# Second layer's gates and banded queries as two by two blocks with seven products

## What is computed

```python
def mixer_odd(h, hc, w_in, w_out, ml_gate_b, ml_norm_g, sw_sink, need_ctx):
    pl = split_cols(h @ w_in, ODD_SPLITS)
    pc = split_cols(hc @ w_in, ODD_SPLITS)
    ...
    oc_lat, oc_ctx = bidir_prefix(mlstm_scan, lat_f, ctx_f, lat_b, ctx_b, st0)
    yc = head_rmsnorm(oc_lat, ml_norm_g) * jax.nn.silu(pl[3])
    qd = axial_rope(heads(pl[5], SW_HEADS), rows, cols)
    kd = axial_rope(heads(pl[6], SW_KV_HEADS), rows, cols)
    ...
    od = swa_attn(qd, kd, vd, kdc, vdc, sw_sink)
    yd = merge(od) * jax.nn.silu(pl[8])
    y_lat = jnp.concatenate([yc, yd], axis=-1) @ w_out
```

## Time and profile before

| what | value |
|---|---|
| median of 3 runs | 1600.25 us (1599.61 to 1601.06) |
| profiled execution, span | 1600.2 us |
| PE busy | 1515.5 us (95%) |
| VectorE busy | 757.7 us (47%) |
| ScalarE busy | 570.1 us (36%) |
| GpSimd busy | 35.8 us (2%) |

### The profile page before, as it was taken

How to read it: one execution, slowest core, us unless ns; L and a number is a source line. 1 busy time by engine, 2 the same in 40 slices (tenths; PEclk the granted TensorE clock), 3 DMA queues, 4 the chain that set the end, 5 groups by cost and what they waited for, 6 DMA issues and landing times.

```text
span 1600.2 us, 25568 instructions
## 1 busy us (share of the span) xinstructions
PE 1515.5 (95%) x9656; PEld 1039.9 (65%) x9656; DVE 757.7 (47%) x1653; ACT 570.1 (36%) x1320; POOL 35.8 (2%) x108
## 2 busy tenths in 40 slices
PE   7999989999899899898999999999999999999996
PEld 4675876577467577564588866468574555556985
DVE  3144555423222322332577856245555655665776
ACT  0134355433332322443202342223334555554033
POOL 0000000000000000000000000000000010011000
PEclk9999999999999999999999999999999999999999
DMA  9200020240421412500334511222120200001443
GB/s 379 96 27 14 14 104 22 81 157 28 167 83 60 148 70 78 183 14 15 118 120 159 200 66 54 76 72 63 56 80 25 107 14 14 15 27 35 171 158 125
DMA packets 72037, 139.80 MB, mean 87 GB/s; under 512 B 6656, under 2 KB 44588, under 8 KB 70572
## 3 DMA queue, kind: packets, MB, share of 16 engines
q1 hardware_dynamic: 66604, 135.55, 24.0%
q10 hardware_dynamic: 5312, 2.62, 0.6%
HBM read 125.43 MB, written 12.71 MB: 86 GB/s over the span
## 4 chain that ended last, share of the span: by engine, by line
PE 76%; DVE 9%; issue 9%; ACT 4%; DMA 1%; SPq 0%; POOL 0%; DVEq 0%; ACTq 0%; POOLq 0%
PE proj L1250 16%; PE mixed L1250 14%; PE mixed L1234 4%; PE proj L1237 4%; PE turned L1358 4%; PE mixed L1200 4%; PE turned L1340 4%; PE proj L1234 3%; PE scores L1200 2%; ACT vstage L2095 2%; PE scores L1318 2%; PE mixed L1237 2%; PE scores L1321 2%; ACT work L2095 1%; PE scores L1250 1%
## 5 line engine op out<-in xcount | busy, mean ns | idle before, releaser
L1250 PE MATMUL proj<-hT,weights 128*128 128x512 f32 (+1 forms) x752 | 314.3, 564 | 3.0 <-ACT vstage L2095 2.1
L1250 PE MATMUL mixed<-hT,weights 128*128 128x512 f32 (+1 forms) x672 | 259.1, 534 | 1.5 <-DMA weights<-in_weights 0.9
L1250 PEld LDWEIGHTS proj<-hT,weights 128*128 128x128 f32 x752 | 138.3, 192 | 132.0 <-issue 128.2
L1250 PEld LDWEIGHTS mixed<-hT,weights 128*128 128x128 f32 x672 | 125.4, 194 | 100.6 <-issue 93.8
L2095 ACT ACTIVATE work<-turned 128x512 f32<-128x512 f32 (+2 forms) x136 | 72.7, 534 | 145.9 <-PE turned L1340 106.9
L1794 DVE TENSOR_TENSOR yT<-turned,work 128x128 f32<-128x128 f32 x72 | 21.0, 291 | 159.3 <-PE turned L1358 135.0
L2095 ACT ACTIVATE work<-work,stat 128x640 f32<-128x640 f32 (+8 forms) x98 | 74.0, 755 | 31.8 <-DVE stat L1765 29.8
L1340 PE MATMUL turned<-consts,work 128*128 128x128 f32 (+3 forms) x448 | 69.1, 282 | 10.9 <-DVE yT L1794 8.6
L1340 PEld LDWEIGHTS turned<-consts,work 128*128 128x128 f32 (+3 forms) x448 | 48.6, 139 | 42.9 <-issue 19.1
L1234 PE MATMUL mixed<-weights,hT 128*128 128x256 f32 x320 | 71.1, 379 | 0.0
L1234 PEld LDWEIGHTS mixed<-weights,hT 128*128 128x128 f32 x320 | 60.2, 190 | 9.0 <-issue 1.2
(11 more groups left out here) (343 smaller groups left out, 2590.1 us busy)
## 6 DMA issues: line engine op xcount, KB each, us to landing
weights<-in_weights SPq DMA_DIRECT2D x130, 512.0 KB, 3.9
tables<-in_bias SPq DMA_DIRECT2D x8, 1281.0 KB, 6.6
pair<-in_weights SPq DMA_DIRECT2D x20, 512.0 KB, 6.9
hT<-in_xT SPq DMA_DIRECT2D x8, 640.0 KB, 16.0
yT<-in_weights SPq DMA_DIRECT2D x8, 512.0 KB, 8.5
work<-in_xT SPq DMA_DIRECT2D x16, 256.0 KB, 2.8
x1T<-yT SPq DMA_DIRECT2D x8, 512.0 KB, 3.0
work<-rows SPq DMA_DIRECT2D x32, 128.0 KB, 3.4
```

What stands on the lines that cost most here:

```text
L1250: last = nc.tensor.matmul(PJ[BANK_OF[u]][:, 0:n], weights[:, w % WBUFS, k, :], src[:, k, t0:t0 + n], start=(k == 0), stop=(k == KT - 1))
```

## The change

The 12 tiles are taken in six pairs (`TILE_PAIRS`). For a pair, the weights A are two by two blocks (one tile by half the input features), the tokens B likewise (half the features by 512 tokens), and the four quarters of the result come out of seven products of 4 matmuls each, in the order 1, 6, 2, 7, 5, 4, 3, in place of eight. Product 1 is kept by ScalarE (`upper`), 6 and 7 are added to it on VectorE (`upper`, `lower`), 2 is accumulated in PSUM onto 1, and 3 onto 5; for the late gates 4 is accumulated onto 7. Sums of tokens (`token_parts`, `token_last`) are made once for all pairs and kept on chip, in `tables`, the context columns of `yT`, the end of `pair` and `gate_w`; sums of weight tiles (`tile_sum`) are made for each pair, two in place and two in `work`. A gate quarter is multiplied in `quarter_gated`, which stands later in the list than the product. A query quarter is rotated as before, with the scale moved from ScalarE to VectorE's multiplications. The filling of the scan is reordered: keys, values and shared values in the first head pair, the shared keys, then the first three pairs; attention has the last three, and its last steps have no filling. One transfer of an output tile (tile 4) is issued later.

The diff, cut to what counts:

```diff
+TILE_PAIRS = ((("gate", 1, 4), ("gate", 1, 5)), (("gate", 1, 6), ("gate", 1, 7)), (("sw", 0, "q"), ("sw", 1, "q")),
+              (("gate", 1, 0), ("gate", 1, 1)), (("sw", 2, "q"), ("sw", 3, "q")), (("gate", 1, 2), ("gate", 1, 3)))
+PRODUCTS = (1, 6, 2, 7, 5, 4, 3)
+QUARTER_OF = {2: (0, 0), 5: (1, 1), 4: (1, 0), 3: (0, 1)}
...
     for s in main:
+        if s[0] == "lin_turn" and both_banks():
+            out += units[done]
+            done += 1
...
+def pair_products(g, following=None):
...
+    for m in PRODUCTS:
+        steps = [("pair", g, m, part, slot[m], stage.get(m)) for part in range(2)]
+        late = {7: 2, 4: 5, 3: 4}.get(m)
+        gated = [("quarter_gated", g, late, stage[late])] if late and gate else []
+        out += steps[:1] + gated + steps[1:]
+        if m == 7:
+            out.append(("tile_sum", g, 3))
+        if following is not None and m in (5, 4):
+            out += [("tile_sum", following, x) for x in ((0, 1) if m == 5 else (2,))]
+    return out + ([("quarter_gated", g, 3, stage[3])] if gate else [])
...
-    first = k[:4] + g[8] + k[4:8] + g[9] + k[8:] + v
-    vv = project(("sw", 0, "v"), "vv", CHUNKS_ALL)
-    third = vv[:4] + g[13] + vv[4:8] + g[10] + vv[8:] + g[11] + rq[0][:5] + g[14] + rq[0][5:] + g[15]
-    s += scans(1, [first, project(("sw", 0, "k"), "kk", CHUNKS_ALL) + g[12], third])
-    last = attention(1, [rq[1] + g[0], rq[2] + g[2], rq[3] + g[4], g[5] + g[7]], [g[1], g[3], g[6]])
+    vv, kk = project(("sw", 0, "v"), "vv", CHUNKS_ALL), project(("sw", 0, "k"), "kk", CHUNKS_ALL)
+    first = k[:4] + v[:8] + k[4:8] + vv[:4] + k[8:] + v[8:] + vv[4:]
+    for x in range(4):
+        first.insert(12 + 8 * x, ("token_parts", 1, x))
+    second = kk + [("tile_sum", 0, x) for x in range(3)]
+    pairs = [pair_products(g, g + 1 if g + 1 < len(TILE_PAIRS) else None) for g in range(len(TILE_PAIRS))]
+    s += scans(1, [first, second[:-3], second[-3:] + [("token_last", 1)] + pairs[0] + pairs[1] + pairs[2]])
+    (one, two), (three, four) = cut_after(pairs[3], 11), cut_after(pairs[5], 3)
+    four, five = cut_after(four, 7)
+    last = attention(1, [one, pairs[4], four, []], [two, three, five])
...
+            def s_pair(g, m, part, u, stage):
+                left = {1: one[:, 0:4], 6: sum_two, 2: one[:, 4:8], 7: two[:, 0:4], 5: sum_one, 4: two[:, 4:8], 3: one[:, 4:8]}[m]
...
+                    if m == 6:
+                        pe.wait_ge(*at(("token_parts", 1, 3)))
+                        pe.wait_ge(*at(("tile_sum", g, 2)))
...
+                    if m in (6, 5, 4):
+                        right = token_part(m, k)
+                    else:
+                        right = halves(hT[:, k + (4 if m in (2, 3) else 0), half_at(m in (7, 3))])
...
+            def s_token_last(l):
...
+                b12, b22 = (hT[:, f:f + 4, half_at(1)] for f in (0, 4))
+                link(V.tensor_tensor(b12, b22, b12, ALU.subtract), ("token_last", l))
...
+            def rotate(kind, t0, n, st, stage, scale):
...
+                link(V.tensor_tensor(dst, dst, st, ALU.add), ("stage_used", stage), ("rotated", *kind, t0),
+                     *([("filled", "sw", kind[1], "rq")] if (t0 + n == T) != bool(kind[1] % 2) else []))
```

## The result

The changed kernel takes 1609.15 us (median of four runs, 1608.43 to 1611.31), the kernel before 1599.93 beside it: a ratio of 1.007, with a 95% interval of 1.005 to 1.009. It is slower by 9 us by the medians and by 11 us by the ratio, with 24 products less to compute. The interval of the ratio leaves 8 to 14 us. The profiled execution of the changed kernel took 1609.61 us, its span is 1607.8.

The account below looks back on a forecast made before the run. PE was taken as the bound, busy for 1515.5 of 1600.2 us. Saved products gave -20.6 us; waits, clock and attention, less old waits gone, brought the sum to +5.9, so 1606.1 us, range 1590 to 1616.

Parts of the forecast that it names:

- Waits before attention: Scan: new PE waits of 4.3 us in the first pair, 2.4 in the middle, 3.1 and 6.4 at the end.
- -1.8: Scan: two PE waits of 0.8 and 0.9 us for ScalarE before the keys' chunks go.
- some 20: Sign to look for: scan's start to first scores some 20 us longer.
- Clock: Slower clock behind PE waits: 3.4 us behind the first, 3.2 at attention's start, 6.6 together; 2.5 more within attention.
- Attention's waits: Attention: new att_out waits of 9.0 us replace 8.4 of old waits, +0.6 net, bounds -4 and +5.
- 4.3 us against 2.5: Attention, gate pair's product 3 at a step's end: VectorE holds att_out 4.3 us against 2.5 of pv and scores.
- the 15 that I had named as a sign of being wrong: Sign of a wrong forecast: attention's waits grow past 15 us.
- the rival of a cascade: Attention: each held att_out delays the next step and drops the clock, +4.5 us waits, +2.5 clock, 1613 us; chance 0.14.
- VectorE keeps pace: Query pair: first wait, scan's end and their clock shrink together; 1584.8 us all gone, 1595.5 half gone; chance 0.17.
- it decides at a VectorE chain of 5.0 and 6.9 us: Test of the VectorE rival: chain of 5.0 us before the first pair's product 6, 6.9 behind the query pair's product 5.
- The clock stays: Rival: no clock loss behind the waits, so without 6.6, 2.5 and 0.9 the time is 1596.1 us; chance 0.13.
- It doesn't do what it says: Rival: products with moving side in two pieces of 256 columns run slower than 0.859 us; 1.4 us per 1%; chance 0.01.

Follow-up runs that it names:

- e1: Changed kernel with the first pair's three tile sums moved ahead of the last chunk of the shared keys: 1605.66 us, ratio 1.0046 to the kernel before.
- e10: Changed kernel with the edits of e1 and e4, plus pair 3's first product moved from attention to the scan's end: 1586.29 us, ratio 0.9929.
- e12: Kernel before with only the scan's filling reordered, products left whole: 1599.89 us, ratio 1.0026.
- e2: Changed kernel with the query pair second and the two late early-gate tiles third: 1608.78 us, ratio 1.0061.
- e8: Changed kernel with the edits of e1 and e4, plus the scan's fifteen tile sums on GpSimd instead of VectorE: 1597.61 us, ratio 1.0000.
- e7: Changed kernel with attention's tiles (pairs 3 to 5) computed as whole chunks again, some values left wrong: 1613.06 us, ratio 1.0099.
- e6: Changed kernel with unused matmuls, 5 ahead of the first pair's product 6 and 7 ahead of the first scores: 1607.52 us, ratio 1.0057.
- e9: Changed kernel with the edits of e1 and e4, plus unused matmuls, 3 ahead of the last turn and 6 ahead of the first scores: 1595.24 us, ratio 0.9987.
- e4: Changed kernel with the last gate multiplications of pairs 3 and 5 in attention queued behind the next softmax maxima: 1605.33 us, ratio 1.0034.

## Why the forecast was right, and where it was off

I had put the time at 1606.1, with slower at 0.58. It is 1609.15. The mechanism and its places are right, and several terms of the sum were too small: from the scan's start to the end, after's profiled execution is 14.9 us longer than before's (592.8 against 577.9), where the sum has 5.9. That the number came out within 3 us of the median is in part luck, as the last point below shows.

- **Waits before attention.** Forecast and measured in after: 4.3 and 4.33 for the third tile sum; 3.1 and 3.26 before the last turn; 6.4 and 6.21 before the first scores; in the middle 0.9, 0.6 and 0.9, measured 0.94, 0.57 and 0.92. These came out of counting 0.72 us for each 512-wide operation in a strict queue. e1 takes the first away by order alone, e10 the last by giving TensorE other work, so both are waits for VectorE's queue. My sum had slips here: its own terms for the chain ahead of the scores add up to 13.1, not 13.2, and so to a wait of 6.2.
- **The filling.** "-1.8" for two waits that go was right, but I checked only ScalarE's copies there. The new order makes one for VectorE's copy, 2.6 us (e12), with 1.7 us of missing clock behind it in after. This term was missing. The scan grew by 25.0 us; without these 4.3 it is 20.7, against "some 20".
- **Clock.** The row that I took, 3.15 us idle and 3.4 missing, counts idle time too; of TensorE's busy time 3.1 were missing there, and 2.9 are missing behind the first wait. Behind the last turn I had nothing, and 1.5 are missing. Of attention's 8.1 some 2.1 stand at its start, where I had 3.2; for the rest I took 2.5, and 6.0 are missing, behind waits of 2.1 and 3.5 us and at the end. In all it is 14.3 in place of 9.1 (1.7 of it behind the values' wait), the largest mis-sized term.
- **Attention's waits.** I had att_out held for 1.8, 1.1 and 2.4 by the gate pairs and for 1.0 and 2.7 by the query pair. Measured are 0.5, 2.7, 1.0, 2.1 and 3.5, 9.9 in place of 9.0. The step that was off is "4.3 us against 2.5": VectorE was still at the two multiplications of the quarter before when product 3 ended (1319.9), and came to its sum at 1320.77, 0.9 us late. ScalarE's waits rose from 4.5 to 8.3, which I had not counted. Steps without filling take 4.7, not 4.46. All of PE's waits in attention, the first scores left out, come to 21, over the 15 that I had named as a sign of being wrong; the rival of a cascade holds in that part. Attention came out 8.7 us shorter, where I had said 10 to 16.
- **What balanced it.** The medians are 9.2 us apart, the changed stretches of the two profiled executions 14.9 with the end. Such a gap is within what the clock does to single executions (the first stretch alone scatters by 8.4). In the first stretch the profiled execution of before misses 13.3 us of clock and that of after 6.1, which is where 7 us of the 14.9 went in the two spans. The mean granted clock of every execution is on record: over the whole span, the kernel before misses some 17 us in the mean (82 executions), after 29.7 in its four. That is 13 us more, as the stretches have it, and over the 9.1 of the sum. By the ratio the loss is 11 us where the sum has 5.9, so the sum had about half of it, and the range was wide. The medians and ratios stand for the kernels, the profile for the places.

The rivals. *VectorE keeps pace* is false as I put it: the waits stood where the sum had them, and moving the query pair (e2) only moved them. e8, which takes 15 operations off VectorE, can't decide, as GpSimd holds VectorE meanwhile; e7 shows that three sums less shorten the wait before the scores by 2.1 us. But "it decides at a VectorE chain of 5.0 and 6.9 us" was the right test, and e1 and e10 pass it from the other side, by an earlier start and by more cover. *The clock stays* is false in its first half, the dips are there; its price of 6.6 us is within the scatter of two medians (e6, e9: about 2 us each by the ratio). *It doesn't do what it says* is false: the eight passes of a product take 3.60 us with the drain (e10's row at 1244.19), which is 8 times 0.43 and 0.17.

## What to carry to other kernels

Products saved on the engine that is the bound can be paid for in latency on the engine that combines them. Count for each product who needs its combination next, and what stands ahead of it in that engine's queue. Where such a wait remains, look for independent work of the bound engine that can be issued ahead of it, before trying to make the other engine faster: here one product moved ahead of a wait (e10) gave 11.7 us by the ratio, against 3.8 and 5.8 for each reordering of VectorE's queue (e1, e4) and nothing for handing its sums to GpSimd (e8), each uncertain by a few us. An operation that waits for a third engine goes behind those whose operands are there (e4). A moved chunk needs a look at the bank that it shares with its successor, on whichever engine copies it out (e12).

## What the hardware showed that I had not expected

- The same 6455 matmuls of the first stretch take 1015.0 to 1023.4 us in the profiled executions, and missing clock there goes with it, from 5.8 to 13.5 us. It comes in pieces of 1.7 or 3.4 us, at places that recur (near 215, 415 and 1008 us), now one and now the other and at some places not in every execution. So what a wait costs in clock differs from one execution to the next, and one profile shows only one case of it. The Trainium skill (TensorE: Matmul & The Clock Gate, Part 1) says that the moment of the change is not tied to the kernel's start, so that the same kernel sees it at different places from run to run. The first stretch agrees.
- GpSimd's 128x512 sum takes 1.27 us (up to 1.82 where the two engines meet) where VectorE's takes 0.69, and holds VectorE's operations with two SBUF operands: 1.75 and 1.64 in place of 0.69 (e8).
